# Down projections of a split-fp32 SwiGLU: five residual steps, finer signals, fewer double slots

## The reference

```
D_MODEL, D_FF, SEQ = 2048, 5632, 256
def swiglu(h, wg, wu, wd):
    return (jax.nn.silu(h @ wg) * (h @ wu)) @ wd
...
x = x + 0.5 * swiglu(rmsnorm(x, ffn1_norm[i]), ffn1_wg[i], ffn1_wu[i], ffn1_wd[i])
x = x + hybrid_mixer(...)
x = x + 0.5 * swiglu(rmsnorm(x, ffn2_norm[i]), ffn2_wg[i], ffn2_wu[i], ffn2_wd[i])
```

## Time and profile before

| | |
|---|---|
| median of three runs | 1873.33 us |
| the profiled execution | 1874.4 us, span 1872.6 us |
| TensorE busy | 1824.8 us (97%), 8176 matmuls and transposes |
| VectorE busy | 1486.6 us (79%) |
| ACT busy | 1000.3 us (53%) |
| DMA | 367.05 MB, mean 196 GB/s |
| mean granted TensorE clock | 0.995 |

### The profile page before, as it was taken

How to read it: one execution, slowest core, us unless ns; L and a number is a source line. 1 busy time by engine, 2 the same in 40 slices (tenths; PEclk the granted TensorE clock), 3 DMA queues, 4 the chain that set the end, 5 groups by cost and what they waited for, 6 DMA issues and landing times.

```text
span 1872.6 us, 23493 instructions
## 1 busy us (share of the span) xinstructions
PE 1824.8 (97%) x8176; PEld 1493.7 (80%) x8176; DVE 1486.6 (79%) x1767; ACT 1000.3 (53%) x1302; POOL 245.8 (13%) x442
## 2 busy tenths in 40 slices
PE   9999999999999999999999999999999999999997
PEld 7888887778888777888788888888887778888775
DVE  6788887787888787678677856788887788888786
ACT  7455554444555455556567636455555445555454
POOL 1111211001111100000133200111111001111100
PEclk9999999999999999999999999999999999999999
DMA  7767766557676656766443655676765556766653
GB/s 256 203 200 219 214 195 210 177 181 224 202 210 216 191 172 194 216 203 203 146 139 99 215 190 187 198 214 200 219 216 192 186 184 203 224 202 204 229 185 124
DMA packets 199271, 367.05 MB, mean 196 GB/s; under 512 B 19012, under 2 KB 23856, under 8 KB 199056
## 3 DMA queue, kind: packets, MB, share of 16 engines
q1 hardware_dynamic: 185008, 352.37, 60.8%
q0 software_dynamic: 11648, 12.02, 2.1%
q10 hardware_dynamic: 2528, 1.52, 0.3%
HBM read 350.11 MB, written 4.19 MB: 189 GB/s over the span
## 4 chain that ended last, share of the span: by engine, by line
PE 81%; DVE 12%; DMA 5%; ACT 1%; issue 1%; ACTq 0%; DVEq 0%
PE ps L722 21%; PE ps L724 21%; PE ps L723 21%; PE ps L740 5%; PE ps L742 5%; PE ps L741 5%; DMA raw<-in_ffn_wd_dram 5%; DVE w_lo L1736 4%; DVE wt_lo L1811 2%; PE ps L784 2%; DVE wt L1801 1%; ACT w_hi L1236 1%; DVE wt L1804 1%; DVE wt L1806 1%; DVE w_lo L1819 1%
## 5 line engine op out<-in xcount | busy, mean ns | idle before, releaser
L1736 DVE TENSOR_TENSOR w_lo<-raw,w_hi 128x1024 fp32r<-128x1024 f32 x587 | 711.1, 1227 | 247.8 <-ACT w_hi L1236 245.2
L1236 ACT ACTIVATE w_hi<-raw 128x1024 fp32r<-128x1024 f32 x587 | 608.6, 1056 | 474.9 <-PE ps L742 222.5
L722 PE MATMUL ps<-w_hi,hT_hi 128*128 128x512 f32 x1436 | 563.0, 392 | 4.9 <-DVE w_lo L1736 4.9
L724 PE MATMUL ps<-w_hi,hT_lo 128*128 128x512 f32 x1436 | 560.1, 390 | 0.0
L723 PE MATMUL ps<-w_lo,hT_hi 128*128 128x512 f32 x1436 | 559.7, 390 | 0.0
L663 POOL DMA_DIRECT2D gu_raw<-gu_sq x352 | 187.8, 542 | 1114.9 <-DVE gu_sq L1953 1037.8
L722 PEld LDWEIGHTS ps<-w_hi,hT_hi 128*128 128x128 f32 x1436 | 270.1, 188 | 60.6 <-DVE w_lo L1736 6.4
L724 PEld LDWEIGHTS ps<-w_hi,hT_lo 128*128 128x128 f32 x1436 | 269.8, 188 | 57.1
L723 PEld LDWEIGHTS ps<-w_lo,hT_hi 128*128 128x128 f32 x1436 | 270.1, 188 | 55.1
L1287 ACT ACTIVATE wt_hi<-wt 128x1024 fp32r<-128x1024 f32 x136 | 144.4, 1062 | 148.0 <-DVE wt L1801 121.8
L722 PE MATMUL ps<-w_hi,guT_hi 128*128 128x512 f32 x480 | 189.9, 396 | 18.7 <-DVE w_lo L1736 18.7
(11 more groups left out here) (302 smaller groups left out, 2072.5 us busy)
## 6 DMA issues: line engine op xcount, KB each, us to landing
raw<-in_ffn_wu_dram SPq DMA_DIRECT2D x176, 512.0 KB, 4.3
raw<-in_ffn_wd_dram SPq DMA_DIRECT2D x176, 512.0 KB, 4.7
raw<-in_ffn_wg_dram SPq DMA_DIRECT2D x175, 512.0 KB, 4.5
raw<-in_w_in_dram SPq DMA_DIRECT2D x88, 512.0 KB, 3.8
raw<-in_w_out_dram SPq DMA_DIRECT2D x32, 512.0 KB, 4.4
gu_raw<-gu_sq POOLq DMA_DIRECT2D x352, 32.0 KB, 3.5
x_parked<-x SPq DMA_DIRECT2D x8, 256.0 KB, 5.1
raw<-in_cmp_k_w_dram SPq DMA_DIRECT2D x8, 256.0 KB, 3.0
```

The source lines that it names most:

```text
L722: mm(o, x_hi, w_hi[:, s, kk, :], start=begin, stop=False, skip_group_check=skip)
L724: ins = mm(o, x_lo, w_hi[:, s, kk, :], start=False, stop=last and kk == GK - 1, skip_group_check=skip)
L1236: act.activation(w_hi[:, c % SLOTS, :, :], raw[:, c % SLOTS, :, :], ACT.Copy).then_inc(hi_ready, 1)
L1736: tt(w_lo[:, s, :, :], raw[:, s, :, :], w_hi[:, s, :, :].bitcast(F32), ALU.subtract).then_inc(lo_ready, 1)
```

## The change

- `DOWN` has a table for each half. Double slots per half: 3, 3 in part 0, then 2 and 1 in part 1 (before 4, 4, 3, 3); rows that were in a double slot are plain LEFT and RIGHT slots. The first double slot of a half stands at 6 (before 4); in the last half the only one stands at 9. `QUADS` goes from [4, 3] to [3, 2], and the loops over chunks have one turn fewer, with that chunk as straight-line code.
- `left_residual` takes a step: 0 adds banks 0 and 1, and waits first for ACT's copy of product 1; 1 to 3 form z and add it on the left; 4 adds it on the right. The steps stand behind five slots in a row (`left_steps`), at the turn into chunk 6 behind its slots 0, 1, 2, 3 and 7. The right banks of part 0 have a function and a semaphore of their own (`right_residual`, `right_read`), and stand two slots later.
- `seven_products` adds 1 to `group_done` after the 6th matmul and 1 after the 15th, and signals its end with `pair_done`, which now guards `wt` and product 1. `wt_lo` has a semaphore, `t_lo_ready`, for which TensorE waits twice. Products 5 and 7 come ahead of the one of the second tile. ACT and VectorE split the second tile before the second half of `wt`.
- In part 1 `x_square` and `final_gains` of the first columns move from slot 20 to 23, and the first eight transposes of `x` from slot 19 to 22.

```
-QUADS = [4, 3]
+QUADS = [3, 2]
...
-DOWN = [[(LEFT, 0), (LEFT, 2), (LEFT, 4), (LEFT, 6), (PAIR, 1), (PAIR2, 1), (LEFT, 8), (LEFT, 9),
-         (RIGHT, 0), (PAIR, 3), (PAIR2, 3), (RIGHT, 2), (RIGHT, 4), (RIGHT, 6), (PAIR, 5), (PAIR2, 5),
-         (LEFT, 10), (LEFT, 11), (RIGHT, 8), (RIGHT, 9), (PAIR, 7), (PAIR2, 7), (RIGHT, 10), (RIGHT, 11)],
-        [(LEFT, 0), (LEFT, 2), (LEFT, 4), (LEFT, 6), (PAIR, 1), (PAIR2, 1), (LEFT, 7), (RIGHT, 0),
-         (RIGHT, 2), (PAIR, 3), (PAIR2, 3), (RIGHT, 4), (LEFT, 8), (LEFT, 9), (PAIR, 5), (PAIR2, 5),
-         (RIGHT, 6), (RIGHT, 7), (RIGHT, 8), (RIGHT, 9)]]
+HALF0 = [(LEFT, 0), (LEFT, 2), (LEFT, 4), (LEFT, 6), (LEFT, 7), (LEFT, 8), (PAIR, 1), (PAIR2, 1),
+         (LEFT, 9), (RIGHT, 0), (RIGHT, 2), (RIGHT, 4), (RIGHT, 6), (PAIR, 3), (PAIR2, 3), (RIGHT, 7),
+         (LEFT, 10), (LEFT, 11), (RIGHT, 8), (RIGHT, 9), (PAIR, 5), (PAIR2, 5), (RIGHT, 10), (RIGHT, 11)]
+DOWN = [[HALF0, HALF0],
+        [[(LEFT, 0), (LEFT, 2), (LEFT, 4), (LEFT, 5), (LEFT, 6), (LEFT, 7), (PAIR, 1), (PAIR2, 1),
+          (RIGHT, 0), (RIGHT, 2), (RIGHT, 4), (RIGHT, 5), (LEFT, 8), (LEFT, 9), (PAIR, 3), (PAIR2, 3),
+          (RIGHT, 6), (RIGHT, 7), (RIGHT, 8), (RIGHT, 9)],
+         [(LEFT, 0), (LEFT, 2), (LEFT, 3), (LEFT, 4), (LEFT, 5), (LEFT, 6), (LEFT, 7), (LEFT, 8),
+          (LEFT, 9), (PAIR, 1), (PAIR2, 1)] + [(RIGHT, q) for q in (0, 2, 3, 4, 5, 6, 7, 8, 9)]]]
+HALF = [len(DOWN[part][0]) for part in range(2)]
...
+def left_end(part, h):
+    return max(p for p, (kind, _) in enumerate(DOWN[part][h]) if kind in (LEFT, PAIR2)) + 1
+def last_pair(part, h):
+    return max(p for p, (kind, _) in enumerate(DOWN[part][h]) if kind == PAIR)
+def left_steps(part):
+    return {h * HALF[part] + left_end(part, h) + 2 + k: (h, k) for h in range(NDC // 2) for k in range(5)}
...
+X0_AT = 22
+TURN_STEPS = [0, 1, 2, 3, 7]
...
+                no = pair_no(f, c)
                 pe.wait_ge(lo_ready, count(c + 1, i, CHUNK_SLOTS))
                 if first and job:
                     pe.wait_ge(prod_free, count(job, i, 1))
                 product(PROD1, x(0, 0), w(0, 0), first, last)
-                product(0, x(1, 0), w(0, 1), stop=last)
-                pe.wait_ge(lo_ready, count(c + 2, i, CHUNK_SLOTS))
-                product(2, sm(4), w(1, 1), start=first)
+                product(0, x(1, 0), w(0, 1), stop=last).then_inc(group_done, 1)
+                pe.wait_ge(t_lo_ready, count(2 * no + 1, i, 2 * PAIRS))
                 product(PROD5, sm(1), d(T1), first, last)
                 product(PROD7, sm(3), d(T3), first, last)
+                pe.wait_ge(lo_ready, count(c + 2, i, CHUNK_SLOTS))
+                product(2, sm(4), w(1, 1), start=first).then_inc(group_done, 1)
+                pe.wait_ge(t_lo_ready, count(2 * no + 2, i, 2 * PAIRS))
                 product(PROD6, sm(2), d(T2), first, last)
-                product(1, x(1, 1), d(T4), stop=last).then_inc(group_done, 2)
+                product(1, x(1, 1), d(T4), stop=last).then_inc(pair_done, 1)
...
-                                pe.wait_ge(resid_done, resid(stage, NDC - 1))
+                                pe.wait_ge(right_read, NT * (2 * f + 2))
...
-                        if p == at_[0]:
-                            if h:
-                                pe.wait_ge(resid_done, resid(stage, 2 * h - 1))
-                                if f == 0 and part == 1:
+                        if p == at_[h][0]:
+                            if h and part == 0:
+                                pe.wait_ge(right_read, NT * (2 * f + 1))
+                            elif h:
+                                pe.wait_ge(resid_done, resid(R_FFN2B if f else R_FFN1B, 1))
+                                if f == 0:
                                     for b in range(2):
                                         pe.wait_ge(free[4 + b], operand_use(1, b, 0) + 1)
                             else:
                                 pe.wait_ge(gu_done, 2 * chunks_done)
...
-                with pe.Fori(0, PARTN[0] - 3) as i:
+                with pe.Fori(0, QUADS[0] - 1) as i:
                     chunk(2, i)
-                chunk(PARTN[0] - 1)
+                for n in range(QUADS[0] + 1, PARTN[0]):
+                    chunk(n)
...
                 if kind == PAIR2:
+                    hi_pair2(c, i)
                     wt_high(f, c - 1, 1, i)
-                    hi_pair2(c, i)
                 else:
                     hi(c, i, CHUNK_SLOTS)
...
-                act.wait_ge(group_done, count(done, i, CHUNK_SLOTS))
+                act.wait_ge(pair_done, count(pair_no(f, last) + 1, i, PAIRS))
...
-                            for n, g1 in enumerate((20, 25, 39)):
+                            for n, g1 in enumerate((23, 25, 39)):
...
-                if i is not None:
-                    before = c - 3 if (c - FFN0[f]) % CHUNK_SLOTS == PAIRS_AT[1] else c - 9
-                    dve.wait_ge(group_done, count(before, i, CHUNK_SLOTS))
-                elif c != FFN0[f] + PAIR_SLOTS[0]:
-                    dve.wait_ge(group_done, FFN0[f] + PAIR_SLOTS[PAIR_SLOTS.index(c - FFN0[f]) - 1] + 2)
+                if no:
+                    dve.wait_ge(pair_done, count(no, i, PAIRS))
...
                 if kind == PAIR2:
                     s = c % SLOTS
-                    wt_low(f, c - 1, 1, i)
                     dve.wait_ge(hi_ready, count(c + 1, i, CHUNK_SLOTS))
                     tt(w_lo[:, s, 1, :], raw[:, s, 1, :], w_hi[:, s, 1, :].bitcast(F32),
                        ALU.subtract).then_inc(lo_ready, 1)
+                    wt_low(f, c - 1, 1, i)
...
+            def left_residual(f, part, h, step):
...
+                if step == 0:
+                    dve.wait_ge(group_done, FFN0[f] + down_slot(part, h) + left_end(part, h))
+                    dve.wait_ge(prod1_copied, job + 1)
+                    for t in range(NT):
+                        stt(out=x[:, t, cols], in0=ps[:, t, :], scalar=0.5, in1=x[:, t, cols], op0=ALU.mult,
+                            op1=ALU.add).then_inc(left_read, 1)
+                elif step == 1:
+                    dve.wait_ge(left_read, done + 2)
+                    add(0)
+                    tt(z[:, 1, :], ps[:, PROD6, :], z[:, 1, :], ALU.add).then_inc(prod_d, 1)
+                elif step == 2:
+                    dve.wait_ge(prod_d, job + 1)
+                    tt(z[:, 0, :], ps[:, PROD5, :], z[:, 1, :], ALU.add).then_inc(prod_f, 1)
+                    tt(z[:, 1, :], ps[:, PROD7, :], z[:, 1, :], ALU.add).then_inc(prod_e, 1)
+                elif step == 3:
+                    dve.wait_ge(prod_e, job + 1)
+                    add(1)
+                    last_sum(f, key)
+                else:
+                    dve.wait_ge(prod_free, job + 1)
+                    right = x[:, :, n * CH + CH:n * CH + 2 * CH]
+                    stt(out=right, in0=z[:, :, :], scalar=0.5, in1=right, op0=ALU.mult,
+                        op1=ALU.add).then_inc(prod_used, 1)
+                    dve.wait_ge(prod_used, job + 1)
+                    if part == 1:
+                        dve.sem_inc(resid_done, NT)
+            def right_residual(f, h):
+                dve.wait_ge(group_done, FFN0[f] + down_slot(0, h) + HALF[0])
+                cols = slice((2 * h + 1) * CH, (2 * h + 2) * CH)
                 for t in range(NT):
-                    stt(out=x[:, t, cols], in0=ps[:, t, :], scalar=0.5, in1=x[:, t, cols], op0=ALU.mult,
-                        op1=ALU.add).then_inc(left_read, 1)
-                dve.wait_ge(prod1_copied, job + 1)
-                dve.wait_ge(left_read, done + 2)
-                add(0)
-                product_sums(f, key)
-                add(1)
-                last_sum(f, key)
-                dve.wait_ge(prod_free, job + 1)
-                right = x[:, :, n * CH + CH:n * CH + 2 * CH]
-                stt(out=right, in0=z[:, :, :], scalar=0.5, in1=right, op0=ALU.mult, op1=ALU.add).then_inc(prod_used, 1)
-                dve.wait_ge(prod_used, job + 1)
-                dve.sem_inc(resid_done, NT)
+                    stt(out=x[:, t, cols], in0=ps[:, 2 + t, :], scalar=0.5, in1=x[:, t, cols], op0=ALU.mult,
+                        op1=ALU.add).then_inc(right_read, 1)
+                dve.wait_ge(right_read, NT * (2 * f + h + 1))
...
+                            if p in TURN_STEPS:
+                                left_residual(f, 0, 1, TURN_STEPS.index(p))
+                            if p == 4:
+                                right_residual(f, 1)
...
+                        if g in steps_at:
+                            left_residual(f, part, *steps_at[g])
+                        if part == 0 and g == HALF[0] + 4:
+                            right_residual(f, 0)
```

(42 more changed lines are left out.)

60 lines of the change are left out of this document (28 added, 32 removed).

## The result

The changed kernel takes 1825.61 us (median of 4 runs, 1824.58 to 1827.09), the kernel before 1874.34 in the runs now at hand (1872.37 to 1876.43). The ratio is 0.974, 95% interval 0.9724 to 0.9757. The profiled spans are 1872.6 and 1824.6 us: 48.0 less.

The account below looks back on a forecast made before the run. TensorE, busy 97% with 81% of the chain, bounds the kernel by its work and its waits on VectorE. -24.9 - 17.8 - 2.9 - 7.1 + 6.8 + 2.0 = -43.9 us: median 1873.33 to 1829.4 us, range 1826.5 to 1844.

Parts of the forecast that it names:

- Reading the loss from windows: TensorE's lost time in four windows of the down jobs, against its pitch in full chunks: together 53.9 us.
- Part 2: Residual in five steps: seven long turn waits and the one at the end go, -24.9 us.
- Part 3: Signals within a double slot: its waits, 17.8 us, go; 0.1 us kept at each of 18, 2.0 us left.
- the last 1.2: Remainder of the job windows' 53.9 us loss that the named waits, restarts and clock, 52.7, did not cover.
- Part 1: Ten fewer double slots in the jobs: 30 matmuls more on TensorE, +6.8 us; VectorE gets some 45 us less work.
- Part 4: Two more TensorE waits per double slot, 116 in all: 0, with bounds 0 and 12.8 us.
- Rival B: The extra waits on TensorE cost 0.11 us each, 12.8 us in all: 1842 us, chance 0.07.
- Part 5: Stretches at granted clock 0.50 and restarts behind TensorE's waits: all 7.1 and 2.9 us go.
- Part 6: Four more chunks as straight-line code: 0; bound one tile landing, 4.7 us, a chunk, 19 us.
- Rival C: Code comes late in the unrolled chunks, 19 us: 1848 us, chance 0.03.
- Rival D: Slower: `wt_lo` becomes a wait in all 58 double slots, chunks included, net +27 us: 1900 us, chance 0.04.
- Rivals A and E: A: VectorE stays behind after the turn, 1847 us, chance 0.13. E: new waits keep the eight long ones, 1864, 0.05.

Follow-up runs that it names:

- a_tables_only: Changed kernel with neither the residual steps nor the signals, so only tables, quads and loops differ from the kernel before: 1858.21 us.
- a_nosig: Changed kernel with the signals, waits and order of a double slot as before; new tables and residual steps kept: 1826.74 us.
- a_burst: Changed kernel with all five residual steps at one place, behind the slot where step 0 stands; tables and signals as changed: 1834.24 us.
- a_best: Changed kernel with 4, 4 and 3 double slots in the first three halves, at slots 6, 10, 16, 20 and 5, 10, 14; last half as changed: 1821.38 us.
- b_order: Kernel before with only the order and waits of a double slot as changed; ring slots still free with the 21st matmul: 1863.17 us.
- a_more: Changed kernel with 4, 4, 3 and 2 double slots a half instead of 3, 3, 2 and 1; steps and signals as changed: 1833.58 us.
- b_sig: Kernel before with the signals, waits and order of a double slot as changed; tables and residual burst as before: 1838.41 us.
- b_early: Kernel before with only the early release of ring slots, after the 6th and 9th matmul of a double slot; order and waits as before: 1850.07 us.
- steps_oldtables: Five residual steps with the signals of before and the old tables in the first three halves, one double slot in the last: 1843.61 us.

## Why the prediction came out as it did

- **Reading the loss from windows, 53.9 us: right, and it was the whole answer.** 53.9 us gone and 30 matmuls more (6.8) make -47.1. The spans differ by 48.0. Of the other 0.9, 0.4 lies before the first job and 0.3 between the first block's jobs and the second's.
- **Part 2, -24.9 for the turns: right.** All eight waits went, and with step 0 at E + 0.9 as timed. But the forecast put the whole on the steps, and their share depends on the rest: between a_tables_only and a_nosig, without the signals, they are worth 31.5 us; between a_burst and the changed kernel, with them, 8.6. The signals are worth 24 us with the new tables and no steps, 17 with the steps and the old tables, and nothing that can be told with both.
- **Part 3, "I take 0.1 us each, 2.0 us left": this step failed.** Nothing was left: TensorE has no wait in the jobs. The working had over 2 us of lead at each double slot and the trace shows 3.4 to 4.6; a margin of 2.0 (18 x 0.1 is 1.8) was put on top without a row for it. The same goes for "the last 1.2 is too finely spread to name", which I let stand: it went too, as the windows are full; what it consisted of stays open. 2.0, 1.2 and the 0.9 above are the 4.1 us between -43.9 and -48.0.
- **The range failed with them.** Its bottom was given as "nothing left, and 1 of the unnamed", 1826.5, but the bound from the windows was 1873.3 - 53.9 + 6.8 = 1826.2, and even this lies above the 1825.61 measured: runs of the changed kernel spread by over 1 us to either side (1824.58 to 1827.09). The median of the kernel before alone moved by 1.0 with more runs.
- **Part 1, +6.8 for fewer double slots: right in size, but the reason for paying it was only half right.** They are a source of lead (a_tables_only), but with the signals in place the lead is there without them: a_best has 18 matmuls fewer and no wait in its jobs. That its tables would do without the signals is not shown. The forecast didn't ask for which edits stand in for each other.
- **Part 4, the extra waits on TensorE, 0: right.** 116 of them, and the windows are full. Twelve of them lie in the first job, from its first matmul to that of the next chunk: it takes 126.49 us with them and 126.48 without (a_nosig), where 12 x 0.11 would be 1.3. Rival B is out.
- **Part 5, the clock: right.** 1.00 to the end of the jobs.
- **Part 6, straight-line code, 0: right.** The window from 410 to 600 holds a chunk that was in the loop before. It has 840 matmuls, as it had. That more code comes by DMA can be seen in the page's list of queues, before and after (packets, MB, share):

```profile
q8 instruction: 53, 0.87, 0.2%
...
q8 instruction: 59, 0.97, 0.2%
```

No wait comes of it. The Trainium skill (Advanced Engine Details and Errata, ISA Cache) gives the instruction cache as 32 KB, and 128 KB on TensorE; no run here shows its size. Rival C is out.
- **Rival D, slower by `wt_lo`:** no wait for it anywhere. Rivals A and E would have left waits at double slots or at the turns, and there are none.

## What to carry to other kernels

When one engine has nearly all the chain, count what its stretches would take at its undisturbed pitch: the shortfall is the most that removing waits can give, and the best estimate if each wait has slack by the working. Don't keep a margin that no row asks for, and let the range reach that bound and a run's spread beyond it. Edits that give the same engine lead stand in for each other: after such a change, take each one back, above all the one that costs the bounding engine work. What limits density is the resource with one copy, here `wt`, and a chain row that starts right behind its last reader, after a long idle time, names it.

## What the runs showed of the hardware

While TensorE still had work, the granted clock fell to 0.50 in these profiles only in or just behind waits of 2.2 us and more (before, a_tables_only, b_order, a_more, the ends of b_sig and b_early), and not behind those of up to 1.2 us in b_early or of 1.9 us in steps_oldtables. The three executions of steps_oldtables without a profile had mean clocks of 0.997 and 0.998 against 0.999 in the profiled one, so it may have fallen there; no trace shows where. The shortest wait that brought it stands at 334.3 us in a_tables_only, with the window behind it:

```profile
334.26 0.50 PE L742 MATMUL ps<-w_hi,guT_hi 128*128 128x512 f32 x1 [2.25 <-DVE w_lo L1761]
...
335.30:338.70 3.40, 3.40 (x10) 0.50 0.80 245
```

Whether a given wait brings it is not fixed: of the turn waits of 2.4 us it did so at three of seven in the profile of the kernel before and at all seven in that of b_order, and of those of 2.2 to 2.4 us in a_tables_only at three of eight. Executions of one and the same kernel differ too: the kernel before had mean clocks of 0.991 to 0.997.

A wait on TensorE whose signal has come costs nothing that can be seen (126.49 and 126.48 us for the first job with and without the added ones). In the undisturbed jobs a matmul of 512 columns takes 0.2267 us (558 in 126.49). The Trainium skill (TensorE: Matmul & The Clock Gate, Back-to-back issue gap) has about 216 ns for an isolated one and about 131 ns sustained; neither is met here, and the measurement decides.
